# Latent attention: values stationary in the column halves of TensorE, softmax sums by GpSimd

## The chip, the cores and the metric

The kernel runs on one NeuronCore of a Trainium2 chip. Its engines are TensorE (PE in the profile; PEld is its weight load), VectorE (DVE), ScalarE (ACT), GpSimd (POOL) and the sync engine (SP), which here issues the loads of the weights. The metric is the device time of one execution in microseconds.

## The reference, cut to what matters

Two transformer blocks over 512 tokens of width 1024. The change lies in the latent attention of the second block: 16 heads, keys of 64 + 32 features, values of 64, no mask.

```python
def attend(qblk):
    s = jnp.einsum("bqhd,bkhd->bhqk", qblk, kf, preferred_element_type=jnp.float32) * scale
    pr = jax.nn.softmax(s, axis=-1)
    return jnp.einsum("bhqk,bkhd->bqhd", pr.astype(v.dtype), v)
...
o = jnp.moveaxis(o, 0, 1).reshape(bsz, seq, C_HEADS * C_V)
return o @ w_out
```

## The kernel before

Every engine has a program written out by hand in its order, and the engines meet at semaphores. Most matrices are held as a high and a low part (fp32r), and one `product` is three matmuls of 512 columns (L574 to L576). A panel of weights comes in by a DMA, ScalarE writes its high part (`split`, L1343) and VectorE its low part (`low`, L1963).

The latent attention is a loop over 16 heads n; two heads are a pair p. For a head, on TensorE:

- `maxima(n)`: four matmuls q by k (L887), one for each 128 queries. VectorE takes the row maxima (`largest_of`, L2542) and negates them (L2546, semaphore `negm_ready`).
- `turn(n)`: the negated maxima are transposed to a row (L892). VectorE spreads it into four spare rows of q (`shift_of`, L2551, semaphore `shift_ready`), so that the product itself subtracts the maximum.
- `scores(n, kt)`: one product for each of four tiles kt of 128 keys; keys on the partitions, 512 queries in the row. ScalarE takes the exponential into one of four buffers (`weights_of`, L1604).
- `values(n, kt)`: four matmuls (L915). The weights of 128 queries are stationary, the values of the head (64 columns and a column of ones, which gives the softmax sum) move. The result has queries on the partitions.
- VectorE multiplies by the reciprocal of the sum (`result`, L2561 and L2563). For each pair, `turn_pair` transposes four tiles (L925) so that features lie on the partitions; ScalarE and VectorE split that into h_hi and h_lo (`pair_high`, `pair_low`) for the output projection OUT3.

Between these stand the projections of the next heads. In an even head: `project_nope` (three products, then `nope_of` on ScalarE and `nope_lower`, L2942, on VectorE) and `project_k` (two products, then `k_of` and `k_lower`, L2948). In a head with n % 4 == 1: `project_quad` (three products, then `quad_rope`, L2954 to L2957, and in the next head `quad_lower`). GpSimd only copies the rotated parts to their places.

The work of head n + 1 up to its row of maxima is put into head n, so the scores of head n + 1 wait for `shift_ready`, and that waits for the reductions of head n + 1.

## Time and profile before

| | |
|---|---|
| median of 3 runs | 1940.69 us (1940.3 to 1943.07) |
| the profiled execution | 1942.67 us |
| its span, first to last instruction | 1940.8 us |
| mean granted clock of TensorE | 0.987 |
| PE busy | 1887.3 us (97%) |
| DVE busy | 1133.5 us (58%) |
| ACT busy | 737.3 us (38%) |
| POOL busy | 96.6 us (5%) |
| the 16 heads of the latent attention | 1376.5 to 1532.3 us of the span |

The busy time of PE is the union of its instructions; a matmul's record lasts longer than the step to the next one, since matmuls are pipelined. What a matmul costs is read from the starts of two that follow each other. A float32 matmul has two records, an fp32r matmul one. In timelines, "x8" is a run of eight records of one form, and the first two numbers are the start and the length of the run.

### The profile page before, as it was taken

How to read it: one execution, taken by the hardware profiler on the slowest of the kernel's cores; microseconds unless marked ns; L12 is line 12 of the kernel's file. 1: busy time of each engine (PE TensorE's matmuls, PEld its weight loads, DVE VectorE, ACT ScalarE, POOL GpSimd, SP SyncE). 2: the span in 40 equal slices, each digit the busy share in tenths (PEclk: the TensorE clock that was granted, in tenths of full speed). 3: DMA queues.
4: the chain of work that ended last, by engine and by line, in shares of the span. 5: the costliest groups of instructions: out<-in, count | busy, mean ns of one | idle time of the engine just before them, and what ended most of it. 6: DMA issues, size and time to landing. Idle time of an engine off the chain costs nothing.

```text
span 1940.8 us, 25097 instructions
## 1 busy us (share of the span) xinstructions
PE 1887.3 (97%) x9170; PEld 1562.1 (80%) x9170; DVE 1133.5 (58%) x1637; ACT 737.3 (38%) x1074; POOL 96.6 (5%) x123
## 2 busy tenths in 40 slices
PE   8999999999999999999999999999999999999998
PEld 6787778888888887877788888887788878888887
DVE  7767654784764777676543434476767454444344
ACT  5355222542432454554332322343444343323231
POOL 0020000300000020000000000003111000000000
PEclk9998999999999999999999999999999999999999
DMA  5232003233333332311333333332101133232332
GB/s 208 87 128 90 1 20 112 66 96 96 94 95 96 98 109 87 98 55 33 92 92 96 95 97 97 97 97 80 52 22 34 34 97 95 94 96 96 97 98 87
DMA packets 47929, 165.70 MB, mean 85 GB/s; under 512 B 5216, under 2 KB 7264, under 8 KB 47712
## 3 DMA queue, kind: packets, MB, share of 16 engines
q1 hardware_dynamic: 46368, 161.27, 26.3%
q10 hardware_dynamic: 1472, 3.22, 0.5%
q8 instruction: 58, 0.95, 0.2%
q14 instruction: 31, 0.25, 0.0%
HBM read 162.38 MB, written 2.10 MB: 85 GB/s over the span
## 4 chain that ended last, share of the span: by engine, by line
PE 87%; DVE 7%; ACT 2%; POOL 1%; issue 1%; DMA 0%; DVEq 0%; ACTq 0%; POOLq 0%
PE ps L574 26%; PE ps L576 25%; PE ps L575 25%; PE ps L915 3%; PE ps L816 2%; DVE w_lo L1963 1%; POOL x L521 1%; PE ps L1159 1%; PE ps L780 1%; ACT w_hi L1343 1%; PE ps L887 1%; DVE tmp L2000 1%; DVE qk_c L2657 0%; DVE mx L2464 0%; PE ps L1119 0%
## 5 line engine op out<-in xcount | busy, mean ns | idle before, releaser
L1343 ACT ACTIVATE w_hi<-raw 128x1024 fp32r<-128x1024 f32 x281 | 297.7, 1059 | 805.0 <-PE ps L576 804.8
L574 PE MATMUL ps<-h_hi,w_hi 128*128 128x512 f32 (+1 forms) x1288 | 510.5, 396 | 10.7 <-DVE w_lo L1963 9.9
L576 PE MATMUL ps<-h_hi,w_lo 128*128 128x512 f32 (+1 forms) x1288 | 500.1, 388 | 0.0
L575 PE MATMUL ps<-h_lo,w_hi 128*128 128x512 f32 (+1 forms) x1288 | 500.1, 388 | 0.0
L1963 DVE TENSOR_TENSOR w_lo<-raw,w_hi 128x1024 fp32r<-128x1024 f32 x281 | 345.3, 1229 | 126.8 <-ACT w_hi L1343 125.2
L574 PEld LDWEIGHTS ps<-h_hi,w_hi 128*128 128x128 f32 x1288 | 243.5, 189 | 64.5 <-issue 13.9
L575 PEld LDWEIGHTS ps<-h_lo,w_hi 128*128 128x128 f32 x1288 | 243.5, 189 | 50.4 <-issue 2.6
L576 PEld LDWEIGHTS ps<-h_hi,w_lo 128*128 128x128 f32 x1288 | 243.2, 189 | 50.5
L574 PE MATMUL ps<-hid_hi,w_hi 128*128 128x512 f32 (+1 forms) x716 | 273.7, 382 | 1.7 <-DVE w_lo L1963 0.9
L576 PE MATMUL ps<-hid_hi,w_lo 128*128 128x512 f32 (+1 forms) x716 | 272.6, 381 | 0.0
L575 PE MATMUL ps<-hid_lo,w_hi 128*128 128x512 f32 (+1 forms) x716 | 272.6, 381 | 0.0
L2162 DVE TENSOR_TENSOR x<-x,ps 128x512 f32<-128x512 f32 (+2 forms) x82 | 55.3, 674 | 195.6 <-PE ps L576 195.4
L574 PEld LDWEIGHTS ps<-hid_hi,w_hi 128*128 128x128 f32 x716 | 134.6, 188 | 28.8 <-DVE w_lo L1963 2.0
L576 PEld LDWEIGHTS ps<-hid_hi,w_lo 128*128 128x128 f32 x716 | 134.6, 188 | 25.9
L575 PEld LDWEIGHTS ps<-hid_lo,w_hi 128*128 128x128 f32 x716 | 134.6, 188 | 25.8
L2845 DVE SCALAR_TENSOR_TENSOR ev<-ps,tmp 128x512 f32<-128x512 f32 x64 | 44.3, 692 | 161.0 <-PE ps L576 157.1
L915 PEld LDWEIGHTS ps<-mla_v,c_raw 128*128 128x128 f32 x512 | 65.4, 191 | 5.5 <-issue 0.8
L1604 ACT ACTIVATE c_raw<-ps 128x512 f32<-128x512 f32 x64 | 38.2, 597 | 67.9 <-PE ps L576 67.8
L915 PE MATMUL ps<-mla_v,c_raw 128*128 128x65 f32 x512 | 64.0, 268 | 0.0
L1623 ACT ACTIVATE pr<-ps 128x512 f32<-128x512 f32 x48 | 28.1, 597 | 79.8 <-PE ps L806 79.6
L2464 DVE TENSOR_REDUCE mx<-ps 128x1 f32<-128x512 f32 (+4 forms) x52 | 29.8, 587 | 32.9 <-PE ps L784 20.4
L2542 DVE TENSOR_REDUCE mla_mx<-ps 128x1 f32<-128x512 f32 x64 | 41.1, 685 | 13.3 <-PE ps L887 12.8
(381 smaller groups left out, 2379.2 us busy)
## 6 DMA issues: line engine op xcount, KB each, us to landing
raw<-in_panels SPq DMA_DIRECT2D x296, 512.0 KB, 3.5
x_in<-in_x SPq DMA_DIRECT2D x8, 256.0 KB, 5.9
x<-in_x ACTq DMA_DIRECT2D x1, 2048.0 KB, 8.4
out<-y SPq DMA_DIRECT2D x16, 128.0 KB, 1.8
first<-in_first SPq DMA_DIRECT2D x1, 1568.0 KB, 11.8
second<-in_second ACTq DMA_DIRECT2D x1, 512.0 KB, 3.6
small<-in_small ACTq DMA_DIRECT2D x1, 332.0 KB, 4.1
masks<-in_masks SPq DMA_DIRECT2D x1, 256.0 KB, 12.0
```

The costliest lines, as they stand in the source:

```text
L574: nc.tensor.matmul(out, a[0], b[0], start=start, stop=False)
L575: nc.tensor.matmul(out, a[0], b[1], start=False, stop=False)
L576: return nc.tensor.matmul(out, a[1], b[0], start=False, stop=stop)
L816: last = nc.tensor.matmul(ps[:, 6 + n // 6, n % 6 * 65:n % 6 * 65 + 65], pr[:, m % 4, h * P:(h + 1) * P], v, start=w["kt"] == 0 and n in ( ...
L915: last = nc.tensor.matmul(ps[:, mla_bank(n), t * 65:(t + 1) * 65], mla_pr[:, m % 4, t * P:(t + 1) * P], mla_v[:, kt, n, :], start=kt == 0 ...
L1343: nc.scalar.activation(w_high(panel, i), raw[:, panel % 4, :], ACT.Copy).then_inc(w_hi_ready, 1)
L1604: nc.scalar.activation(mla_pr[:, m % 4, :], ps[:, 4 + m % 2, :], ACT.Exp, scale=96 ** -0.5).then_inc(exp_done, 1)
L1963: signal(V.tensor_tensor(w_low(panel, i), raw[:, panel % 4, :], w_high(panel, i).bitcast(F32), ALU.subtract), w_lo_ready, wait=False)
L2162: signal(V.tensor_tensor(x[:, k, at], x[:, k, at], bank, ALU.add), done)
L2464: signal(V.tensor_reduce(mx[:, u["n"] % 2, a:a + r["heads"]], ps[:, 2 + at % 2, 0:r["heads"] * keys].rearrange("p (a b) -> p a b", a=r["he ...
L2542: signal(V.tensor_reduce(mla_mx[:, n % 2, t:t + 1], ps[:, 2 + t % 2, :], AX.X, ALU.max), mx_done, wait=False)
L2845: signal(V.scalar_tensor_tensor(ev[:, k % 4, :], bank, 0.0, inv_b, ALU.max, ALU.mult), tile_out, wait=False)
```

## The change

For a pair and a key tile, four matmuls now hold the values (128 keys by 64 features) stationary and let the weights of 256 queries move. The first head of the pair writes partitions 0 to 63 of the result (column half 0 of the array), the second partitions 64 to 127. The result has features on the partitions at once, so `turn_pair` and the column of ones go. The softmax sums come another way: GpSimd adds the four weight tiles of each head (three additions of 128x512), `totals(p)` multiplies the sum by a stationary block of ones (four matmuls, which spread it over 64 partitions), and VectorE turns that by blocks, takes 16 reciprocals for each partition and turns them back (`shares`), then multiplies (`pair_result`). Weights have eight buffers. `values` of a pair runs in its odd head and, for the last key tile, in the next even head. In even heads `turn` stands before the last scores.

```diff
-        def values(n, kt):
-            m = 4 * n + kt
-            pe.wait_ge(exp_done, m + 1)
-            if kt == 0 and n >= 2:
-                pe.wait_ge(o_used, n - 1)
-            for t in range(NT):
-                last = nc.tensor.matmul(ps[:, mla_bank(n), t * 65:(t + 1) * 65], mla_pr[:, m % 4, t * P:(t + 1) * P],
-                                        mla_v[:, kt, n, :], start=kt == 0 and t == 0, stop=kt == NT - 1, skip_group_check=True)
+        def values(p, kt):
+            pe.wait_ge(exp_done, 4 * (2 * p + 1) + kt + 1)
+            if kt == 0 and p >= 2:
+                pe.wait_ge(pair_out, p - 1)
+            for half in range(2):
+                for a in range(2):
+                    n = 2 * p + a
+                    last = nc.tensor.matmul(ps[64 * a:64 * a + 64, pair_bank(p), cols_of(half)], mla_v[:, kt, n, :],
+                                            weights_tile(n, kt)[:, cols_of(half)], start=kt == 0 and half == 0, stop=kt == NT - 1,
+                                            skip_group_check=True)
             last.then_inc(pv_done, 1)
-        def turn_pair(p):
-            pe.wait_ge(o_used, 2 * p + 2)
+        def totals(p):
+            pe.wait_ge(weights_added, 6 * p + 6)
             pe.wait_ge(k_low, min(2 * p + 6, HEADS))
             if p:
-                pe.wait_ge(mix_ready, 8 + p)
-            for t in range(NT):
-                last = nc.tensor.transpose(ps[:, 1, t * P:(t + 1) * P], mla_out[:, p % 2, t, :], ident)
-            last.then_inc(turned, 1)
+                pe.wait_ge(totals_taken, p)
+            for half in range(2):
+                for a in range(2):
+                    last = nc.tensor.matmul(ps[64 * a:64 * a + 64, 1, cols_of(half)], ones[:, 0:64],
+                                            weights_sum(2 * p + a)[:, cols_of(half)], start=half == 0, stop=True, skip_group_check=True)
+            last.then_inc(totals_out, 1)
...
+        def add_weights(n):
+            if n >= 4:
+                pool.wait_ge(totals_out, n // 2 - 1)
+            for kt in range(1, NT):
+                pool.wait_ge(exp_done, 4 * n + kt + 1)
+                nc.gpsimd.tensor_tensor(weights_sum(n), weights_tile(n, 0) if kt == 1 else weights_sum(n), weights_tile(n, kt),
+                                        ALU.add).then_inc(weights_added, 1)
+                pool.wait_ge(weights_added, 3 * n + kt)
...
+            if even and p:
+                values(p - 1, 3)
             scores(n, 1)
             if even and p + 1 < PAIRS:
                 project_nope(p + 1)
-            values(n, 0)
+            if not even:
+                values(p, 0)
             if more:
                 maxima(n + 1, range(2, 4))
             scores(n, 2)
-            if even and p + 1 < PAIRS:
-                project_k(p + 1)
-            if not even and p:
-                turn_pair(p - 1)
-            values(n, 1)
-            scores(n, 3)
-            if more:
-                turn(n + 1)
-            if n % 4 == 1 and p + 2 < PAIRS:
-                project_quad(p // 2 + 1)
-            values(n, 2)
+            if even:
+                if p + 1 < PAIRS:
+                    project_k(p + 1)
+                turn(n + 1)
+                scores(n, 3)
+            else:
+                if p:
+                    totals(p - 1)
+                values(p, 1)
+                scores(n, 3)
+                if more:
+                    turn(n + 1)
+                if n % 4 == 1 and p + 2 < PAIRS:
+                    project_quad(p // 2 + 1)
+                values(p, 2)
...
+            if n >= 2:
+                act.wait_ge(pv_done, 4 * (n // 2 - 1) + kt + 1)
+                act.wait_ge(weights_added, 3 * (n - 2) + max(1, kt))
...
+        def shares(p):
+            dve.wait_ge(totals_out, p + 1)
+            signal(V.transpose(mla_total, ps[:, 1, :]), totals_taken)
+            link(V.reciprocal(mla_w[:], mla_total[:, 0:S:32]))
+            signal(V.transpose(mla_share, mla_w[:].unsqueeze(2).to_broadcast([P, 16, 32])), dve_step)
+
+        def pair_result(p):
+            dve.wait_ge(pv_done, 4 * p + 4)
+            if p >= 2:
+                dve.wait_ge(mix_ready, 8 + p - 1)
+            signal(V.tensor_tensor(mla_out[:, p % 2, :], ps[:, pair_bank(p), :], mla_share, ALU.mult), pair_out, wait=False)
...
-            if n:
-                result(n - 1)
+            if even and p >= 2:
+                pair_low(p - 2)
...
             if not even and p:
-                pair_low(p - 1)
+                shares(p - 1)
+                pair_result(p - 1)
```

On ScalarE, `pair_high(p - 1)` moves behind the last exponential of an odd head, ahead of the `split` of the next panel. At the end of the loop, `totals` of the last pair stands inside the first tile of OUT3, and the second tile is begun before the first one's last product.

In TensorE's program, the end of head 6 and the first instruction of head 7 stood so before; the first two rows are the values of key tile 1, L892 is `turn(7)`, and the last row is the first product of head 7:

```order
L915 MATMUL ps<-mla_v,c_raw 128x65 [waits exp_done]
L915 MATMUL ps<-mla_v,c_raw 128x65 x3
L574 MATMUL ps<-q_hi,k_hi 128x512 [waits exp_done]
L575 MATMUL ps<-q_lo,k_hi 128x512
L576 MATMUL ps<-q_hi,k_lo 128x512
L892 MATMUL ps<-small,mla_negm 4x128 [waits negm_ready]
L915 MATMUL ps<-mla_v,c_raw 128x65 [waits exp_done]
L915 MATMUL ps<-mla_v,c_raw 128x65 x3
L574 MATMUL ps<-q_hi,k_hi 128x512 [waits shift_ready,rope_placed,exp_done,k_low,nope_low]
```

After the change (L598 to L600 is the product, L916 is `turn`), the first two rows are the end of `project_k(4)`:

```order
L599 MATMUL ps<-cq_lo,w_hi 128x512
L600 MATMUL ps<-cq_hi,w_lo 128x512
L916 MATMUL ps<-small,mla_negm 4x128 [waits negm_ready]
L598 MATMUL ps<-q_hi,k_hi 128x512 [waits exp_done]
L599 MATMUL ps<-q_lo,k_hi 128x512
L600 MATMUL ps<-q_hi,k_lo 128x512
L598 MATMUL ps<-q_hi,k_hi 128x512 [waits shift_ready,rope_placed,exp_done,k_low,nope_low]
L599 MATMUL ps<-q_lo,k_hi 128x512
```

Both visits of the values have left the end of the even head, and one product stands between `turn` and the scores that wait for its result.

In VectorE's program, this stood from head 5 (n % 4 == 1) to the second half of head 6 before; L2567 is `pair_low(1)`, L2954 to L2957 `quad_rope`, L1963 the low part of a panel:

```order
L2567 TENSOR_TENSOR h_lo<-ps,h_hi 128x512 [waits turned_high]
L2954 STREAM_SHUFFLE c_t<-ps 128x512 [waits quad_low,quad_proj]
L2955 TENSOR_TENSOR c_t<-ps,trig 128x512 [waits dve_step]
L2956 TENSOR_TENSOR c_t<-c_t,trig 128x512 [waits quad_taken]
L2957 TENSOR_TENSOR c_t<-c_t 128x512 [waits dve_step]
L1963 TENSOR_TENSOR w_lo<-raw,w_hi 128x1024 [waits w_hi_ready,quad_done]
L2542 TENSOR_REDUCE mla_mx<-ps 128x1 [waits mx_ready] x2
L2963 TENSOR_TENSOR quad_lo<-c_t,quad_hi 128x512 [waits rope_placed,quad_high]
L2561 RECIPROCAL mla_w<-ps 128x4 [waits pv_done]
L2563 TENSOR_TENSOR ang<-ps,mla_w 128x4x64 [waits dve_step]
L2942 TENSOR_TENSOR q_lo<-ps,q_hi 64x512 [waits nope_high,o_used]
L2942 TENSOR_TENSOR q_lo<-ps,q_hi 64x512 [waits nope_high]
```

After the change, the same place (L2605 to L2607 are `shares(1)`, L2614 is `pair_result(1)`, L2618 `pair_low`):

```order
L2605 STREAM_TRANSPOSE sq<-ps 128x512 [waits totals_out]
L2606 RECIPROCAL mla_w<-sq 128x16 [waits totals_taken]
L2607 STREAM_TRANSPOSE sq<-mla_w 128x512 [waits dve_step]
L2614 TENSOR_TENSOR ang<-ps,sq 128x512 [waits pv_done,dve_step]
L3005 STREAM_SHUFFLE c_t<-ps 128x512 [waits quad_low,quad_proj]
L3006 TENSOR_TENSOR c_t<-ps,trig 128x512 [waits dve_step]
L3007 TENSOR_TENSOR c_t<-c_t,trig 128x512 [waits quad_taken]
L3008 TENSOR_TENSOR c_t<-c_t 128x512 [waits dve_step]
L2010 TENSOR_TENSOR w_lo<-raw,w_hi 128x1024 [waits w_hi_ready,quad_done]
L2589 TENSOR_REDUCE mla_mx<-ps 128x1 [waits mx_ready] x2
L3014 TENSOR_TENSOR quad_lo<-c_t,quad_hi 128x512 [waits rope_placed,quad_high]
L2618 TENSOR_TENSOR h_lo<-ang,h_hi 128x512 [waits pair_high_ready]
```

Four instructions of 512 columns or fewer now stand ahead of `quad_rope` in the place of `pair_low`, and `pair_low` has taken the place of the two of `result`.

## Rows read from the trace of the kernel before

**Rows 1.** busy times of the stage (engine busy us, instructions; PEclk: granted clock).
```profile
1376.50:1532.30 155.80, 153.32 (x942) 133.51 (x943) 105.55 (x184) 67.25 (x110) 18.22 (x25) 1.00 0.10 31
```

**Rows 2.** waits in the stage: us in total, times, longest.
```profile
PEld ps L574 <- issue: 3.0, 12, 0.3
```

**Rows 3.** timeline of PE, one `values` visit and the product behind it.
```profile
1435.72 1.00 PE L915 MATMUL ps<-mla_v,c_raw 128*128 128x65 f32 x8
1436.53 0.48 PE L574 MATMUL ps<-q_hi,k_hi 128*128 128x512 f32 x1
1436.85 0.39 PE L575 MATMUL ps<-q_lo,k_hi 128*128 128x512 f32 x1
1437.08 0.40 PE L576 MATMUL ps<-q_hi,k_lo 128*128 128x512 f32 x1
```

**Rows 4.** groups by form, whole span: float32 matmuls with 512 and 256 columns.
```profile
L749 PE MATMUL ps<-ret_pr,rv 128*128 128x512 f32 x8 | 4.1, 591 | 0.0
...
L749 PE MATMUL ps<-ret_pr,rv 128*128 128x256 f32 x8 | 2.4, 378 | 0.0
```

**Rows 5.** timeline of PE where 64-row matmuls stand between 128-row ones.
```profile
817.72 0.39 PE L576 MATMUL ps<-w_hi,h_lo 128*128 128x512 f32 x1
818.04 0.46 PE L1107 MATMUL ps<-small,la 64*128 64x64 f32 x4
...
818.59 1.07 PE L1119 MATMUL ps<-neg_m,small 64*128 64x512 f32 x2
819.60 0.50 PE L574 MATMUL ps<-h_hi,w_hi 128*128 128x512 f32 x1
```

**Rows 6.** timeline of PE, the four transposes of `turn_pair`.
```profile
1452.60 0.60 PE L925 MATMUL ps<-small,ang 128*128 128x128 f32 x4
1453.03 1.00 PE L915 MATMUL ps<-mla_v,c_raw 128*128 128x65 f32 x8
```

**Rows 7.** timeline, all engines: head 0 behind its `project_nope`.
```profile
1380.48 1.00 PE L915 MATMUL ps<-mla_v,c_raw 128*128 128x65 f32 x8
...
1382.74 1.29 DVE L2542 TENSOR_REDUCE mla_mx<-ps 128x1 f32<-128x512 f32 x2
...
1384.07 0.17 DVE L2546 TENSOR_SCALAR mla_negm<-mla_mx 128x4 f32<-128x4 f32 x1
```

**Rows 8.** timeline, all engines: from `turn` to the next head's scores.
```profile
1446.45 0.27 PE L892 MATMUL ps<-small,mla_negm 128*4 128x128 f32 x1
...
1446.76 0.68 DVE L2551 TENSOR_TENSOR q_hi<-ps,small 4x512 fp32r<-4x512 f32 x1 [0.39 <-PE ps L892]
...
1447.73 0.47 PE L574 MATMUL ps<-q_hi,k_hi 128*128 128x512 f32 x1 [0.17 <-issue]
```

**Rows 9.** timeline of DVE, from `quad_rope` to the second pair of maxima.
```profile
1395.64 0.73 DVE L2954 STREAM_SHUFFLE c_t<-ps 128x512 f32<-128x512 f32 x1
...
1398.58 1.23 DVE L1963 TENSOR_TENSOR w_lo<-raw,w_hi 128x1024 fp32r<-128x1024 f32 x1
1399.72 1.28 DVE L2542 TENSOR_REDUCE mla_mx<-ps 128x1 f32<-128x512 f32 x2
1400.92 0.68 DVE L2963 TENSOR_TENSOR quad_lo<-c_t,quad_hi 128x512 fp32r<-128x512 f32 x1
...
1402.19 1.41 DVE L2942 TENSOR_TENSOR q_lo<-ps,q_hi 64x512 fp32r<-64x512 f32 x2
1403.63 1.29 DVE L2542 TENSOR_REDUCE mla_mx<-ps 128x1 f32<-128x512 f32 x2
```

**Rows 10.** one line's instructions on GpSimd: duration ns min/median/max.
```profile
L521 POOL TENSOR_TENSOR x<-x,tmp x32: 723/916/929, 339.1 to 728.3; 128x256 f32<-128x256 f32 x32
```

**Rows 11.** one line's instructions on VectorE: duration ns min/median/max.
```profile
L1963 DVE TENSOR_TENSOR w_lo<-raw,w_hi x281: 1209/1225/1572, 7.7 to 1918.0; 128x1024 fp32r<-128x1024 f32 x141
```

**Rows 12.** busy times of two stretches around a fall of the clock.
```profile
170.00:175.00 5.00, 3.25 (x27) 2.79 (x25) 3.01 (x4) 3.01 (x6) 0.00 (x0) 1.00 0.58 204
175.00:180.00 5.00, 4.91 (x14) 2.55 (x12) 4.02 (x7) 2.90 (x6) 0.00 (x0) 0.51 0.33 105
```

More of the change, by code:

```diff
@@ L532, in _ @@
         pool.wait_ge(inv_copied, COPIED_BEFORE["c"] + 1)
-        alone(nc.gpsimd.memset(mla_v[:, :, :, 64:65], 1.0))
         alone(nc.gpsimd.memset(k_hi[:].bitcast(F32), 0.0))
@@ L554, in _, with place_two @@
             alone(nc.gpsimd.tensor_copy(k_lo[rope_rows(n), n, :], k_lo[rope_rows(n), n - 2, :]))
-        for i in range(HEADS // 4):
-            for first in (0, 2):
-                pool.wait_ge(quad_high, i + 1)
-                if i and first:
-                    pool.wait_ge(s_ready, 16 * i)
-                for n in (first, first + 1):
-                    place(q_hi[rope_rows(n), n, :], quad_hi[32 * n:32 * n + 32, :])
-                pool.wait_ge(quad_low, i + 1)
-                for n in (first, first + 1):
-                    place(q_lo[rope_rows(n), n, :], quad_lo[32 * n:32 * n + 32, :])
+        def place_two(i, first):
+            pool.wait_ge(quad_high, i + 1)
+            if i and first:
+                pool.wait_ge(s_ready, 16 * i)
+            for n in (first, first + 1):
+                place(q_hi[rope_rows(n), n, :], quad_hi[32 * n:32 * n + 32, :])
+            pool.wait_ge(quad_low, i + 1)
+            for n in (first, first + 1):
+                place(q_lo[rope_rows(n), n, :], quad_lo[32 * n:32 * n + 32, :])
+        def add_weights(n):
[6 more added lines that the diff above has]
+                pool.wait_ge(weights_added, 3 * n + kt)
+        place_two(0, 0)
+        place_two(0, 2)
+        for n in range(HEADS):
+            if n % 4 == 2 and n + 2 < HEADS:
+                place_two(n // 4 + 1, 0)
+            add_weights(n)
+            if n % 4 == 3 and n + 1 < HEADS:
+                place_two(n // 4 + 1, 2)
         inverse_root("ffn2")
@@ L862, in project_k @@
             if p >= 3:
-                pe.wait_ge(mix_ready, 8 + p - 2)
+                pe.wait_ge(totals_taken, p - 2)
             for k in range(2):
@@ L891, in turn @@
             pe.wait_ge(negm_ready, n + 1)
-            nc.tensor.transpose(ps[0:4, mla_bank(n), 384:512], mla_negm[:, n % 2, :], ident).then_inc(negm_turned, 1)
+            nc.tensor.transpose(ps[0:4, 2, 0:P], mla_negm[:, n % 2, :], ident).then_inc(negm_turned, 1)
         def scores(n, kt):
@@ L1243, in _ @@
             dense(panel, moving=(aq_hi, aq_lo))
-        def out_run(panel, base, most):
-            for k in range(KD):
-                dense(panel + k, freed=k == KD - 1, **(dict(ready=mix_ready, base=base, most=most) if k == 0 else {}))
         def feed_forward(panel, base, hidden, name, halved=None):
@@ L1305, in _ @@
                 maxima(n + 1, range(0, 2))
-            if n:
-                values(n - 1, 3)
+            if even and p:
+                values(p - 1, 3)
             scores(n, 1)
@@ L1314, in _, with out_part @@
             scores(n, 2)
-            if even and p + 1 < PAIRS:
-                project_k(p + 1)
-            if not even and p:
-                turn_pair(p - 1)
-            values(n, 1)
-            scores(n, 3)
-            if more:
-                turn(n + 1)
-            if n % 4 == 1 and p + 2 < PAIRS:
-                project_quad(p // 2 + 1)
-            values(n, 2)
-        values(HEADS - 1, 3)
-        turn_pair(PAIRS - 1)
-        out_run(OUT3, 8, 16)
+            if even:
+                if p + 1 < PAIRS:
+                    project_k(p + 1)
+                turn(n + 1)
+                scores(n, 3)
[9 more added lines that the diff above has]
+                values(p, 2)
+        values(PAIRS - 1, 3)
+        def out_part(panel, ks):
+            pe.wait_ge(w_lo_ready, panel + 1)
+            pe.wait_ge(tile_out, output_of(panel) - 3)
+            for k in ks:
+                pe.wait_ge(mix_ready, 8 + k + 1)
+                last = product(ps[:, bank_at(panel), :], w(panel, k * P, (k + 1) * P), (h_hi[:, k, :], h_lo[:, k, :]), k == 0, k == KD - 1)
+                if k == KD - 1:
+                    last.then_inc(panel_read, 1)
+        out_part(OUT3, range(0, 2))
+        totals(PAIRS - 1)
+        out_part(OUT3, range(2, KD - 1))
+        out_part(OUT3 + 1, range(0, KD // 2))
+        out_part(OUT3, range(KD - 1, KD))
+        out_part(OUT3 + 1, range(KD // 2, KD))
+        for panel in range(OUT3 + 2, OUT3 + KD):
+            dense(panel, freed=panel == OUT3 + KD - 1)
         feed_forward(FF2, 0, sum(FF0_CHUNKS) + 8 * FF_CHUNKS, "ffn2", halved="final")
@@ L2998, in _ @@
                 low(pair_panel(p + 3))
-        result(HEADS - 1)
+        pair_low(PAIRS - 2)
+        shares(PAIRS - 1)
+        pair_result(PAIRS - 1)
         pair_low(PAIRS - 1)
```

58 lines of the change are left out of this document (25 added, 33 removed).

## The prediction

> **What bounds the kernel now.** I read first the busy times of the stage: from the first scores of head 0 to OUT3, PE is busy 153.3 of 155.8 us at a granted clock of 1.00, VectorE 105.6, ScalarE 67.3, GpSimd 18.2 [rows 1]. So PE sets the end, and any PE work that goes is gained, as long as the chains on the other engines still fit under it. The waits show where they nearly don't: twelve times PE's weight load for L574 is held up [rows 2]. One such place: after `turn` the matrix result reaches VectorE 0.31 us later, `shift_of` takes 0.68, and the next head's first product starts 0.29 us after that, 1.28 us after `turn` in all [rows 8]. The values visit in between fills only 0.11 + 0.81 us [rows 3], so each of the twelve costs about 0.36 us, 4.3 in all. The stage is PE bound with a latency chain just under its surface.
>
> **PE work removed.** A values visit takes 0.81 us to the next start, and the product behind it takes one step of 0.32 where 0.23 is usual [rows 3]: 0.90 us, times 64 is 57.6. `turn_pair` takes 0.43 [rows 6] and the same 0.09, times 8 is 4.2. Together 61.8 us.
>
> **PE work added.** There are 32 new visits and 8 `totals`, each four float32 matmuls of 256 columns, eight records. A record of such a matmul lasts 378 ns at 256 columns and 591 at 512 [rows 4]; the difference says that 256 columns stream for 0.213 us. Neighbouring matmuls write different column halves, and nothing before runs two halves of the array at once, so this cost is bounded: all eight in a row are 1.71 us, two halves fully side by side 0.85. In between, if records start in program order, the second record of one matmul runs beside the first of the next: five slots, 1.07. I take 1.07, since the two records of one matmul share a half and PE's records start in order in every timeline that I read. Then the change of tile shape: the one place with another shape is 64 rows, where the first L1107 starts 0.32 after L576 instead of 0.23; the last L1119 streams until about 819.50 (818.59 + 1.07 - 0.59 + 0.43) and L574 starts at 819.60 [rows 5]. That is 0.09 in and 0.09 out, and 0.09 on the product behind as today: 0.28. The other end is 0.09, since the 4-column L892 shows no step [rows 8]. I take 1.35 us a visit: 40 x 1.35 = 54.0. **PE work: 54.0 - 61.8 = -7.8 us** (side by side -16.6, in a row +17.8).
>
> The Trainium skill (TensorEngine Tiling (Array Packing), Tiling Modes, Key Properties) says that different tiles can execute LdWeights and Matmul in parallel, but that changing the mode drains the engine. By its first half alone the saving would be nearer 16.6, by its second each visit pays both ways. The 64-row rows agree with a price of the mode change, 0.09 each way; no row shows two tiles in parallel.
>
> **Waits added in even heads.** This is what speaks against the change. The visits of key tiles 0, 1 and 2 have left the even heads, where the longest chain is. In head 0 the last `project_nope` matmul gives way at 1380.48; then ScalarE, `nope_lower`, two reductions and the negation follow, until 1384.07 + 0.17 [rows 7], 3.76 us, and 0.29 to PE [rows 8]: 4.05. Ahead of `turn` PE had 0.46 + 0.69 + 1.38 us and two visits and a product, 5.0 in all. Now it has 2.53. PE stands 1.5 us at `turn` in heads 0 and 2.
> From head 4 on VectorE is the longer one. From its `shift_of` in an odd head to the next negation it does (steps between starts): `shift_of` 0.71 [rows 8], `shares`, `pair_result` 0.72, `quad_rope` 2.94, low part 1.14, reductions 1.20, `quad_lower` 0.68, `pair_low` 0.72, `nope_lower` 1.44 [rows 9], reductions and negation 1.50 [rows 7]. A block transpose is in no row: I take the shuffle's 0.76 [rows 9], between 0.5 and 1.5, twice, and 0.2 for the reciprocal, 1.72. Sum 12.8, with 0.31 and 0.29 at the ends 13.4. PE in the same stretch: `turn` 0.11, `project_quad` 2.07, two visits 2.70, three products 2.07, `project_nope` 2.07, four maxima 0.92, `project_k` 1.38, 11.3. Wait 2.05, in heads 6 and 10.
> In heads 4, 8 and 12 there is no `quad_rope` and `quad_lower`; but there the low part waits about 1.7, since ScalarE's `split` now stands behind `pair_high`, which waits for `pair_result`: VectorE 11.4, PE 9.25, wait 2.2. Head 14 has no projections: 10.0 against 5.8, wait 4.2. Sum: 3.0 + 4.1 + 6.6 + 4.2 = 17.9.
> Behind `turn` the even head has one product, 0.69. Reckoned from the negation, `k_lower` 0.71, `shift_of` 0.71 and 0.29 stand against 0.29 + 0.11 + 0.69: 0.6 in 8 heads, 4.8. Odd heads have the visit of 1.35 there, which covers 1.28. From 22.7 the 4.3 of before go, and 0.7 at the end of the loop, where `turn_pair` stood alone behind `result` and OUT3 now fills in. **Waits: +17.7 us.**
>
> **GpSimd.** Its addition of 256 columns takes 0.92 us [rows 10]; 512 columns are at most 1.83, at least 1.3. Three for a head and 1.2 us of placements are 6.7 of the 10 us that a head takes, so `totals`, a head and a half later, doesn't wait; behind it on PE stand a visit and the last scores. ScalarE's new waits for GpSimd lie two heads back. But the low part took up to 1.57 us instead of 1.23 [rows 11], the longest ones beside GpSimd's copies. VectorE has 5.9 us of operations with two SBUF inputs in four heads (two low parts, two of `quad_rope`, `quad_lower`, two of `pair_low`); 28% of it, for the 60% of the time that GpSimd works, is 4 us in the stage, of which I put 2.5 on the path (0 to 4.7).
>
> **Sum:** -7.8 + 17.7 + 2.5 = +12.4 us. The profiled execution took 1942.67, 1.9 more than its span and 2.0 more than the median of the runs, so it gives 1955.1, and on the median **1953 us**. A difference of 0.2% (3.9 us) is what can be told from none.
>
> **Rivals.**
> - Halves in a row (0.25): the eight records don't overlap. Visits of 1.99, PE +17.8; VectorE has more time, and every even head's wait falls to the 1.5 of heads 0 and 2 (12, and about 1 in head 14) beside the 4.8: 18, net +13. 1940.7 + 30.8 + 1.5 is 1973. For it: no row shows an overlap. Against: the halves share neither weights nor results.
> - Fully side by side (0.18): PE -16.6, but VectorE bounds six of the even heads, and each waits 0.44 more (two visits): 25.3, net +20.3. With 2.5 for GpSimd, 1947.
> - The clock falls (0.13): the granted clock went to about 0.5 in a stretch behind 5 us in which PE was busy 3.25 [rows 12], and around `turn` in an even head PE will be busy 0.8 of about 3.2 us (1.8 and 0.6 waited). 3.3 us at half speed lose 1.65; eight times is 13: 1966. Against: it is one place, and the odd heads between stay dense.
> - GpSimd becomes the bound (0.05): from additions of about 2.5 us; at 3.0 `totals` waits 5 us more in all: 1958.
> - Not slower (0.12): side by side and no price for the mode change. A visit costs 0.85 + 0.09 = 0.94, PE saves 24, and the waits of net 22 eat it: 1939 to 1943. Faster by over 0.2% it gets below 0.80 us a visit, or where the transposes take 0.5 (2.7 us less) and GpSimd disturbs nothing: 1936.
>
> **How the numbers follow.** The forecast has 0.27, with its own range 1949 to 1961 (transposes, disturbance, mode change). Slower is it and the first four rivals with nearly all of their chance, 0.87; the last splits into 0.06 same and 0.06 faster, and 0.01 of the side-by-side case is same. The range runs from the side-by-side case less 3 us to the serial one plus 3: 1944 to 1976; outside are the last rival and the tails.
>
> **What would show it.** The start of a visit to the next instruction: 1.26 (1.07 and the way in and out), or 1.9 or 0.95, for the halves. Waits of PE's `turn` (L916) for VectorE's negation of 11 us or more and of the maxima (L911) for VectorE's reductions of some 5 us; L598 held for `shift_of` in every even head, never in an odd one. VectorE's busy share in the stage above 70%; additions on GpSimd of 1.5 to 1.8 us; no wait of PE for GpSimd. The stage, 155.8 us before, should last about 168. The forecast is wrong if the visits are not bound by streaming 256 columns, if the clock falls, or if VectorE's stretch between `shift_of` and the negation is not 13 us.

## The result: 0.5% slower, and the profile after

| | before | after |
|---|---|---|
| median | 1940.69 us (5 runs, 1939.11 to 1944.22) | 1950.70 us (5 runs, 1949.65 to 1952.65) |
| ratio | 1 | 1.005, 95% interval 1.0036 to 1.0065 |
| span of the profiled execution | 1940.8 us | 1950.7 us |
| first scores of head 0 to OUT3 | 155.8 us | 164.3 us |

The forecast was 1953 (1944 to 1976), slower with a chance of 0.87. The attention stage grew by 8.5 us, which is nearly the whole difference. The stretch of [rows 1] is now this one (busy us and instructions for PE, PEld, DVE, ACT and POOL, PEclk, DMA share, GB/s):

```profile
1376.40:1540.70 164.30, 145.01 (x711) 90.83 (x711) 113.61 (x180) 66.92 (x110) 77.34 (x73) 0.97 0.10 29
```

PE is busy for 145.0 us of the stage, 8.3 less than before, and it stands idle for 19.3 us where it was 2.5. VectorE has 8.1 us more to do (it is busy for 69% of the stage, where the forecast had said above 70%), GpSimd 59. The granted clock is 0.97 where it was 1.00. PE's work did shrink; what it gave back, and more, went into waits.

**A visit.** Timeline of PE in the kernel after, one visit of `values` with the products around it (start, length, line):

```profile
1533.82 0.39 PE L600 MATMUL ps<-q_hi,k_lo 128*128 128x512 f32 x1
1534.14 0.43 PE L941 MATMUL ps<-c_raw,mla_v 128*64 128x256 f32 x1
1534.14 0.43 PE L941 MATMUL ps<-ev,mla_v 128*64 128x256 f32 x1
1534.40 0.38 PE L941 MATMUL ps<-c_raw,mla_v 128*64 128x256 f32 x1
1534.41 0.38 PE L941 MATMUL ps<-ev,mla_v 128*64 128x256 f32 x1
...
1534.84 0.38 PE L941 MATMUL ps<-c_raw,mla_v 128*64 128x256 f32 x1
1534.84 0.38 PE L941 MATMUL ps<-ev,mla_v 128*64 128x256 f32 x1
1535.15 0.50 PE L598 MATMUL ps<-q_hi,k_hi 128*128 128x512 f32 x1
1535.49 0.40 PE L599 MATMUL ps<-q_lo,k_hi 128*128 128x512 f32 x1
```

The records of the two heads (c_raw and ev) start at the same moment. The next pair starts 0.26 us later, the two behind it (one is left out above) at steps of 0.22, where [rows 4] gave 0.213 for the stream of 256 columns. Eight records take four slots, not the five that I took and not eight. From the first record to the next product are 1.01 us. Around it L941 starts 0.32 behind L600 instead of 0.23, and L599 0.34 behind L598 instead of 0.23: a visit costs 1.01 + 0.09 + 0.11 = 1.21 us.

**The waits.** PE and its weight load in the stage (us in total, times, the longest):

```profile
PE ps L916 <- DVE mla_negm L2593: 11.0, 8, 2.5
...
PE ps L598 <- DVE q_hi L2598: 4.7, 8, 1.0
PE ps L911 <- DVE mla_mx L2589: 4.0, 5, 2.5
...
PEld ps L954 <- POOL tmp L577: 1.8, 5, 0.4
```

Forecast were 17.9 us at `turn` and the maxima together, and 4.8 for `shift_of` (L598). The rows say 11.0 + 4.0 and 4.7. One of the eight waits of L598, the longest with 0.98 us, ends where the stage begins (1376.42) and stood there before the change too; in the stage are seven, 3.7 us.

These rows count idle time, from the end of one record to the start of the next. What a wait costs is more, since the last record lasts longer than its step. One of the waits of `turn`:

```profile
1403.41 0.39 PE L600 MATMUL ps<-cq_hi,w_lo 128*128 128x512 f32 x1
1405.24 0.27 PE L916 MATMUL ps<-small,mla_negm 128*4 128x128 f32 x1 [1.44 <-DVE mla_negm L2593]
```

L916 starts 1.83 us behind L600, where 0.23 is usual: the wait costs 1.60, not 1.44. Counted so over the timeline of the stage, from start to start as the forecast had them, `turn` waits 12.3 us, the maxima 6.6 (the second matmul of a pair is late too) and `shift_of` 4.9, 23.8 in all.

**What was not in the sum: a held negation.** The instructions of one line of the kernel after, the negation of 128x4 maxima (ns: shortest, median, longest):

```profile
L2593 DVE TENSOR_SCALAR mla_negm<-mla_mx x16: 169/170/1178, 1374.6 to 1530.2; 128x4 f32<-128x4 f32 x16
```

Three of the fifteen in the stage are long, 0.45, 1.18 and 1.18 us. A timeline of one of the two longest, cut to GpSimd's addition (L577), the negation and `turn` (L916):

```profile
1447.56 1.26 POOL L577 TENSOR_TENSOR tmp<-tmp,c_raw 128x512 f32<-128x512 f32 x1
1447.67 1.18 DVE L2593 TENSOR_SCALAR mla_negm<-mla_mx 128x4 f32<-128x4 f32 x1
...
1448.90 0.27 PE L916 MATMUL ps<-small,mla_negm 128*4 128x128 f32 x1 [2.49 <-DVE mla_negm L2593]
```

And the chain through it, in order of time:

```profile
1443.79 0.60 DVE quad_lo L3014
1444.39 0.60 DVE h_lo L2618
1444.99 0.59 DVE q_lo L2993
...
1445.62 0.69 DVE q_lo L2993
...
1446.34 1.30 DVE mla_mx L2589 x2
...
1447.67 1.18 DVE mla_negm L2593
```

GpSimd's addition starts at 1447.56 and lasts 1.26 us, to 1448.82. The negation starts 0.11 us later and ends at 1448.85. `turn` (L916), which had been held for 2.49 us, starts at 1448.90. In the kernel with shorter additions (below) no negation of the stage takes more than 172 ns. The chain shows what else stands ahead of it, all VectorE: the low parts of the rotated q, the pair and the next q (L3014, L2618, L2993), two reductions, the negation.

The Trainium skill (SBUF — State Buffer, Who interferes with whom) says that a `tensor_scalar` of VectorE in a mode that uses two ports excludes GpSimd and is excluded by it for a whole instruction, whichever starts first. The row agrees: the negation ends 0.03 us after the addition. No row shows which mode it ran in.

**And the clock.** Three stretches of the stage, the same columns as above:

```profile
1403.00:1407.20 4.20, 2.22 (x10) 1.27 (x9) 4.07 (x7) 1.96 (x4) 2.30 (x3) 1.00 0.00 0
1407.20:1410.70 3.50, 3.50 (x12) 2.21 (x12) 1.30 (x3) 1.20 (x2) 1.06 (x1) 0.51 0.02 5
1445.00:1450.00 5.00, 2.38 (x11) 1.31 (x9) 4.87 (x7) 1.87 (x4) 3.60 (x4) 1.00 0.10 39
```

In 1403.0 to 1407.2 PE was busy for 2.22 of 4.2 us; then the granted clock was 0.51, the lower of its two levels (1.2 of 2.4 GHz), for 3.5 us, which costs 1.7. In 1445 to 1450 PE was busy for 2.38 of 5 us and the clock stayed. Four heads later the same wait of 2.49 us came again, behind the same work (2.39 of 5 us in 1487.1 to 1492.1), and there the clock fell, at 1492.6. So a long wait can bring a fall, but whether one comes can't be told from these rows. In all it fell three times in the stage, 5.1 us; before, never.

### The profile page after: what moved, and what is told of

It reads as the page before. It is cut to its first block, busy times and chain, and to the rows that moved or that the text cites. A ratio compares the mean times of both kernels' runs of the same rounds, so it can differ in the third digit from the quotient of the medians.

```text
span 1950.7 us, 24721 instructions
## 1 busy us (share of the span) xinstructions
PE 1880.6 (96%) x8946; PEld 1519.6 (78%) x8946; DVE 1144.8 (59%) x1637; ACT 737.2 (38%) x1074; POOL 155.8 (8%) x170
## 4 chain that ended last, share of the span: by engine, by line
PE 84%; DVE 11%; ACT 2%; issue 2%; POOL 1%; DMA 0%; DVEq 0%; ACTq 0%; POOLq 0%
PE ps L598 25%; PE ps L600 24%; PE ps L599 24%; PE ps L840 2%; DVE w_lo L2010 1%; PE ps L941 1%; ACT w_hi L1389 1%; DVE mla_mx L2589 1%; POOL x L527 1%; PE ps L1189 1%; PE ps L804 1%; PE ps L911 1%; DVE tmp L2047 1%; DVE q_lo L2993 0%; DVE qk_c L2708 0%
## 5 line engine op out<-in xcount | busy, mean ns | idle before, releaser
L598 PE MATMUL ps<-h_hi,w_hi 128*128 128x512 f32 (+1 forms) x1288 | 510.8, 397 | 10.5 <-DVE w_lo L2010 9.7
L599 PE MATMUL ps<-h_lo,w_hi 128*128 128x512 f32 (+1 forms) x1288 | 500.3, 388 | 0.0
L600 PE MATMUL ps<-h_hi,w_lo 128*128 128x512 f32 (+1 forms) x1288 | 500.2, 388 | 0.0
L598 PEld LDWEIGHTS ps<-h_hi,w_hi 128*128 128x128 f32 x1288 | 243.4, 189 | 65.8 <-issue 14.5
L600 PEld LDWEIGHTS ps<-h_hi,w_lo 128*128 128x128 f32 x1288 | 243.2, 189 | 50.5
L599 PEld LDWEIGHTS ps<-h_lo,w_hi 128*128 128x128 f32 x1288 | 243.5, 189 | 50.0 <-issue 2.6
L598 PE MATMUL ps<-hid_hi,w_hi 128*128 128x512 f32 (+1 forms) x716 | 273.6, 382 | 1.7 <-DVE w_lo L2010 0.9
L599 PE MATMUL ps<-hid_lo,w_hi 128*128 128x512 f32 (+1 forms) x716 | 272.6, 381 | 0.0
L600 PE MATMUL ps<-hid_hi,w_lo 128*128 128x512 f32 (+1 forms) x716 | 272.6, 381 | 0.0
L598 PEld LDWEIGHTS ps<-hid_hi,w_hi 128*128 128x128 f32 x716 | 134.6, 188 | 29.0 <-DVE w_lo L2010 2.0
L600 PEld LDWEIGHTS ps<-hid_hi,w_lo 128*128 128x128 f32 x716 | 134.6, 188 | 25.8
L599 PEld LDWEIGHTS ps<-hid_lo,w_hi 128*128 128x128 f32 x716 | 134.6, 188 | 25.6
L2896 DVE SCALAR_TENSOR_TENSOR ev<-ps,tmp 128x512 f32<-128x512 f32 x64 | 44.3, 692 | 161.1 <-PE ps L600 157.2
L500 POOL TENSOR_TENSOR r<-r,small 128x2 f32<-128x2 f32 x6 | 4.2, 701 | 893.4 <-DVE r L2100 893.4
L495 POOL TENSOR_TENSOR r<-r,small 128x4 f32<-128x4 f32 x8 | 8.1, 1015 | 517.7 <-DVE r L2053 517.7
L598 PE MATMUL ps<-w_hi,h_hi 128*128 128x512 f32 (+1 forms) x128 | 47.1, 368 | 1.5 <-DVE w_lo L2010 1.5
```

The lines of the kernel that those rows point to most:

```text
L598: nc.tensor.matmul(out, a[0], b[0], start=start, stop=False)
L599: nc.tensor.matmul(out, a[0], b[1], start=False, stop=False)
L600: return nc.tensor.matmul(out, a[1], b[0], start=False, stop=stop)
L2896: signal(V.scalar_tensor_tensor(ev[:, k % 4, :], bank, 0.0, inv_b, ALU.max, ALU.mult), tile_out, wait=False)
```

## The experiments

All times are medians; the kernel before ran beside each group of four, at 1940.8 to 1941.1. The stage is read from each profiled execution, as above, and varies less than the whole (no edit touches what is ahead of it, and yet it starts anywhere from 1371.9 to 1377.0). It is one execution for each kernel, and so is the number of falls.

| kernel | median us | ratio to before, 95% | stage us | clock falls in the stage |
|---|---|---|---|---|
| before | 1940.69 | 1 | 155.8 | 0 |
| after | 1950.70 | 1.0050 (1.0036 to 1.0065) | 164.3 | 3 |
| shares first | 1943.76 | 1.0015 (1.0006 to 1.0024) | 157.2 | 1 |
| visit ahead of `turn` | 1950.09 | 1.0050 (1.0038 to 1.0062) | 163.4 | 3 |
| split first | 1951.80 | 1.0056 (1.0044 to 1.0068) | 167.5 | 7 |
| all reordered | 1932.84 | 0.9959 (0.9947 to 0.9971) | 147.6 | 0 |
| few additions | 1945.31 | 1.0021 (1.0012 to 1.0031) | 157.7 | 1 |
| half twice | 1950.60 | 1.0047 (1.0030 to 1.0064) | 166.0 | 4 |
| before, small maxima | 1939.30 | 0.9996 (0.9986 to 1.0006) | 155.8 | 0 |
| after, small maxima | 1939.57 | 0.9987 (0.9977 to 0.9996) | 152.0 | 1 |
| one half | 1975.36 | 1.0181 (1.0164 to 1.0198) | 189.2 | 2 |
| shares and split first | 1942.42 | 1.0013 (1.0002 to 1.0024) | 157.2 | 1 |
| reordered, few additions | 1931.95 | 0.9953 (0.9937 to 0.9970) | 144.9 | 0 |
| before, spare additions | 1940.49 | 1.0000 (0.9990 to 1.0010) | 155.8 | 0 |

A fall lasts 3.4 us and costs 1.7; one of twice that length counts as two. The theory: PE saves some 15 us, and in the even heads the chain of VectorE's operations up to the negation eats it. The rivals: GpSimd's additions, the clock, or a saving on PE that isn't there.

### Does PE save what the timeline says?

**Half twice.** In a visit both matmuls of one head stand ahead of both of the other:

```diff
-            for half in range(2):
-                for a in range(2):
+            for a in range(2):
+                for half in range(2):
```

> In a values visit the loops are exchanged: both 256-column matmuls of one head, then both of the other, so that neighbouring matmuls use the same column half of the array except in the middle. Theory (two halves stream together only where neighbouring matmuls alternate between them): a visit costs some 0.4 to 0.8 us more, 32 visits 13 to 25 us of PE work, partly in stretches that wait anyway, time 1958 to 1970. Rival (PE looks further ahead, or the side by side doesn't matter): 1951.

Measured 1950.60, the rival; the stage is longer by the 1.7 us of one more fall. The timeline of PE shows why:

```profile
1410.41 0.38 PE L941 MATMUL ps<-c_raw,mla_v 128*64 128x256 f32 x1
1410.42 0.43 PE L941 MATMUL ps<-ev,mla_v 128*64 128x256 f32 x1
1410.63 0.38 PE L941 MATMUL ps<-c_raw,mla_v 128*64 128x256 f32 x1
1410.69 0.38 PE L941 MATMUL ps<-ev,mla_v 128*64 128x256 f32 x1
...
1411.43 0.50 PE L598 MATMUL ps<-q_hi,k_hi 128*128 128x512 f32 x1
```

In the code, both matmuls of `c_raw` (four records) stand ahead of the first of `ev`. Yet the first record of `ev` starts 0.01 us behind the first of `c_raw`, and the visit still takes 1.02 us. The two halves stream side by side in either order, so PE's records don't start in the order of the program across the halves. That was the reason for my five slots, and it is wrong. The Trainium skill (TensorEngine Tiling (Array Packing), Tiling Modes, Key Properties) says that different tiles can execute in parallel; both orders agree, with starts 0.00 to 0.06 us apart.

**One half.** Both heads are written to the same 64 rows of the bank (so the output mixes the two heads):

```diff
-                    last = nc.tensor.matmul(ps[64 * a:64 * a + 64, pair_bank(p), cols_of(half)], mla_v[:, kt, n, :],
+                    last = nc.tensor.matmul(ps[0:64, pair_bank(p), cols_of(half)], mla_v[:, kt, n, :],
...
-                    last = nc.tensor.matmul(ps[64 * a:64 * a + 64, 1, cols_of(half)], ones[:, 0:64],
+                    last = nc.tensor.matmul(ps[0:64, 1, cols_of(half)], ones[:, 0:64],
```

> Both heads of a pair are written to the same 64 rows of the bank, so that all matmuls of values and totals use one column half of the array; their number and shapes are those of the change. The output isn't the reference's: two heads are added up in one half, and the other is stale. Theory (the change's PE work is short because the two halves stream at the same time): the eight records of a visit start 0.215 us apart, the visit takes 2.0 us instead of 1.2, 40 visits are 32 us more PE work, of which some 8 to 14 fill stretches in which PE waits for VectorE now; time 1968 to 1975. Rival (the overlap doesn't come from the two halves): 1950 to 1952.

Measured 1975.36, 24.7 above the change and just above the expected range. A visit of it:

```profile
1409.30 0.65 PE L941 MATMUL ps<-c_raw,mla_v 128*64 128x256 f32 x2
1409.78 0.59 PE L941 MATMUL ps<-ev,mla_v 128*64 128x256 f32 x2
1410.21 0.59 PE L941 MATMUL ps<-c_raw,mla_v 128*64 128x256 f32 x2
1410.64 0.59 PE L941 MATMUL ps<-ev,mla_v 128*64 128x256 f32 x2
1411.17 0.73 PE L911 MATMUL ps<-k_hi,q_hi 128*128 128x512 f32 x2
```

Now the eight records follow each other and the visit takes 1.87 us, 0.86 more than 1.01. The stage holds 39 of the 40 (the last `totals` stands in OUT3), so 33.5 us. Shorter waits take 6.1 back (17.7 us from start to start instead of 23.8) and one fall of the clock fewer 1.7, which leaves 25.7; the stage grew by 24.9. So the overlap is worth 0.86 us a visit, and it comes from the two halves.

**Small maxima, before and after.** The row maxima are taken over 32 of the 512 columns, and the exponent's scale is 0.001 instead of 0.102 so that nothing overflows (the output isn't the reference's). That shortens VectorE's chain by some 2 us a head and leaves PE's work alone:

```diff
-                signal(V.tensor_reduce(mla_mx[:, n % 2, t:t + 1], ps[:, 2 + t % 2, :], AX.X, ALU.max), mx_done, wait=False)
+                signal(V.tensor_reduce(mla_mx[:, n % 2, t:t + 1], ps[:, 2 + t % 2, 0:32], AX.X, ALU.max), mx_done, wait=False)
```

> The kernel before with the row maxima taken over 32 of the 512 columns and the exponent's scale made 0.001 instead of 0.102, so that no exponential overflows; the output isn't the reference's. VectorE's chain is shorter by about 2 us a head, PE's work is the same. Theory: before, the chain was already hidden, so 1938 to 1941.

> The change with the same two cuts (row maxima over 32 of 512 columns, exponent's scale 0.001; the output isn't the reference's). Theory (VectorE's chain eats the change's saving of about 15 us on PE): the wait of L916 falls from 11.0 to some 5 us and this runs at or below the kernel before with the same cut: from 4 below it to 1 above, 1936 to 1941. Rival (PE saves little or nothing, as my sum's 7.8, or GpSimd costs it): it stays 5 us or more above the kernel before with the same cut.

The kernel before hardly moves (its stage is 155.8 us with and without), the change gains 11.1 us and is level with it: 1939.57 and 1939.30. In the stage it is 3.7 us ahead. The wait of `turn` fell from 11.0 to 6.3. Of the 12.3 us that the stage gained, 3.4 are two falls of the clock fewer, the rest waits. So there is a saving on PE, and VectorE's chain stood on it; before, that chain was covered.

### Which order loses it?

**Shares first.** In odd heads VectorE does the sums of the last pair and its result ahead of `shift_of`:

```diff
+            if not even and p:
+                shares(p - 1)
+                pair_result(p - 1)
...
-            if not even and p:
-                shares(p - 1)
-                pair_result(p - 1)
```

> Only VectorE's order changes: in odd heads the sums' transposes and the product with the values (shares, pair_result) stand ahead of shift_of for the next head, not behind it. Theory (VectorE's chain in the even heads eats PE's saving): shift_of is the first thing that VectorE does after the odd head's maxima and the rest of the chain to the next negation is VectorE's, so the 2.3 us of shares and pair_result come off it wherever VectorE had been idle ahead of shift_of; the wait of L916 falls from 11.0 to 3 to 6 us, a new wait of L598 for shift_of in odd heads takes up to 1 us back, and the time is about 1944 to 1946, 5 to 6 us below the change. Rival (GpSimd's additions slow VectorE, or the clock falls set the loss): the order doesn't matter and the time stays at 1950 to 1951.

Measured 1943.76, 6.9 less. The total is about right, what makes it up is not what I had expected (PE's waits, in the stage):

```profile
PE ps L916 <- DVE mla_negm L2593: 10.6, 8, 1.8
...
PE ps L598 <- DVE q_hi L2598: 6.4, 12, 0.6
...
PE ps L911 <- DVE mla_mx L2589: 0.3, 1, 0.3
```

`turn` still waits 10.6 us; it is the wait for the maxima that fell from 4.0 to 0.3, and two of the three falls of the clock went, which is 3.4 of the 7.1 us that the stage gained; the waits, from start to start, gave 2.8. The reason is in VectorE's row of `nope_lower` (L2993; the last numbers are its idle time ahead of it and what ended it), first of the change with two rows that are used below, then of this kernel:

```profile
L2010 DVE TENSOR_TENSOR w_lo<-raw,w_hi 128x1024 fp32r<-128x1024 f32 x9 | 12.0, 1335 | 6.7 <-ACT w_hi L1389 6.6
...
L2993 DVE TENSOR_TENSOR q_lo<-ps,q_hi 64x512 fp32r<-64x512 f32 x14 | 9.6, 686 | 3.4 <-ACT q_hi L1928 3.2
...
L2593 DVE TENSOR_SCALAR mla_negm<-mla_mx 128x4 f32<-128x4 f32 x15 | 4.8, 323 | 0.5
```

```profile
L2993 DVE TENSOR_TENSOR q_lo<-ps,q_hi 64x512 fp32r<-64x512 f32 x14 | 9.6, 689 | 10.6 <-ACT q_hi L1928 10.4
```

VectorE now waits 10.4 us there for ScalarE's high part, which waits for PE's own `project_nope`. With VectorE early, the second chain shows: PE, ScalarE, VectorE and back to `turn`, the 1.5 us a head that I had reckoned for heads 0 and 2. Two chains of nearly one length end at `turn`. PE's timeline agrees: `turn` waits 1.15 or 1.16 us in heads 0, 4, 8 and 12 of this kernel, and as long in each of heads 0 to 12 of one half, where PE's own work is longer so what is left there hangs on PE's own work, as the chain through ScalarE does, and not on VectorE alone.

**Visit ahead of `turn`.** In even heads `values(p - 1, 3)` moves from behind the first scores to behind `project_k`:

```diff
-            if even and p:
-                values(p - 1, 3)
...
+                if p:
+                    values(p - 1, 3)
```

> Only PE's order changes: in even heads the visit of key tile 3 goes from behind the first scores to behind project_k, right ahead of the turn. Theory: six of the eight waits are VectorE's length, not PE's, so a visit of 1.2 us put ahead of the turn fills the wait but what stood behind it is missed there, and PE is left to wait for shift_of behind the turn: L916 falls by 7 to 9 us, the wait of L598 grows by about as much, time 1949 to 1951. Rival (the wait at the turn is lost for want of work on PE there): 8 x 1.2 = up to 9 us gained, 1941 to 1943.

Measured 1950.09, no gain. PE's waits in the stage:

```profile
PE ps L911 <- DVE mla_mx L2589: 10.5, 7, 3.7
...
PE ps L916 <- DVE mla_negm L2593: 4.1, 3, 1.5
```

`turn` waits 6.9 us less, and the maxima for VectorE's reductions 6.5 us more. The maxima's second pair stands ahead of `turn`, and the visit had stood ahead of that pair. Without it PE comes to the pair 1.2 us earlier, while VectorE is as late as before: PE meets it there (L911), a step earlier in the head, where I had expected it behind `turn` (L598).

**Split first.** ScalarE splits the next panel ahead of `pair_high`, which waits for VectorE:

```diff
-            if not even and p:
-                pair_high(p - 1)
             if not even and p + 3 <= PAIRS + 1:
                 split(pair_panel(p + 3))
+            if not even and p:
+                pair_high(p - 1)
```

> Only ScalarE's order changes: the split of the next weight panel stands ahead of pair_high (which waits for VectorE's pair_result) in odd heads, not behind it. Theory (chain of VectorE, with its low part late in heads 4, 8, 12 and tight elsewhere): the low part on VectorE no longer waits for the split, L916 falls by 3 to 5 us, time 1946 to 1948. Rival (the split isn't what VectorE waits for): within 1 us of 1950.7.

> Two of the reorderings together: shares and pair_result ahead of shift_of (VectorE), and the split of the next panel ahead of pair_high (ScalarE). Alone the first gave -7 us, with one fall of the clock in its profiled execution, and the second +1 us, with seven falls. Theory (the second shortens the chain too, but alone it left a pattern of waits behind which the clock fell seven times): together 1936 to 1941, with two falls or fewer. Rival (the split wasn't what VectorE waits for): within 1.5 us of the first alone, 1942 to 1945.

Alone 1951.80, 1.1 more than the change; with the shares first 1942.42, against 1943.76 for these alone, intervals that overlap. Both theories fail: no 3 to 5 us came, nor 1936 to 1941. Alone, PE's waits of the three kinds fell a little, from 19.7 to 17.8 us, but `turn` waits more, not less:

```profile
PE ps L916 <- DVE mla_negm L2593: 13.1, 8, 2.5
```

In heads 4, 8 and 12 the wait for the maxima went, so the split was what VectorE had waited for there, and that of `turn` rose from 0.88 to the 1.16 us of the other chain: nearly nothing was left to gain. And the clock fell seven times instead of three in the profiled execution (the longest of its six), 6.8 us more. Here is one of them, in a place where it had held in the change:

```profile
1445.00:1450.00 5.00, 1.99 (x9) 1.06 (x8) 4.87 (x7) 1.78 (x3) 3.01 (x4) 1.00 0.01 3
1450.00:1453.80 3.80, 3.80 (x14) 2.39 (x14) 1.37 (x3) 1.19 (x2) 1.13 (x1) 0.55 0.00 0
```

PE was busy for 1.99 of 5 us ahead of this fall, 2.38 in the change, where it held. That is no rule: with few additions (below) the one fall came behind 5 us with 2.42. With the shares first there was one fall, and the stage is 157.2 us with or without the split.

**All reordered.** These three, and both `k_lower` behind `shift_of`, and `pair_low` at the end of VectorE's work in an even head:

```diff
-            if even and p >= 2:
-                pair_low(p - 2)
...
-            if even and p + 1 < PAIRS:
-                k_lower(2 * p + 2)
...
+                k_lower(2 * p + 2)
...
+            if even and p >= 2:
+                pair_low(p - 2)
```

> All the reorderings together: the visit ahead of the turn, shares and pair_result ahead of shift_of in odd heads, split ahead of pair_high, both k_lower behind shift_of, pair_low at the end of VectorE's work in even heads. No work is added or taken away. Theory (the change saves PE some 15 us by its halves running side by side, and the order of VectorE and PE around the turns loses them again): the waits of L916 and L911 together fall from 15 to under 5 us and the time is 1932 to 1937, below the kernel before (1940.7). Rival (GpSimd's additions and the clock take it): the sum of the waits hardly changes or comes up elsewhere, 1945 or more.

Measured 1932.84, 17.9 below the change and 8 below the kernel before (ratio 0.9959). Its stage in busy times, and PE's waits in it:

```profile
1374.00:1521.60 147.60, 139.66 (x712) 88.59 (x712) 115.93 (x180) 67.26 (x110) 79.41 (x72) 1.00 0.11 33
```

```profile
PE ps L598 <- DVE q_hi L2598: 4.7, 12, 0.6
...
PE ps L916 <- DVE mla_negm L2593: 1.2, 1, 1.2
...
PE ps L911 <- DVE mla_mx L2589: 0.6, 1, 0.6
```

The same work in another order takes 147.6 us: the waits at `turn` and the maxima are 1.8 us instead of 15.0, all of PE's idle time is 7.9 instead of 19.3, and the clock never fell, which is 5.1 of the 16.7 us that the stage gained. The gains don't add up one by one: -6.9, -0.6 and +1.1 alone, -17.9 together. Shares first uncovers the chain through ScalarE, and the visit alone meets VectorE's. But moving `k_lower` and `pair_low` was not tried by itself, so how much is theirs, and how much comes of moving both chains at once, stays open.

### What do GpSimd's additions cost?

**Few additions.** GpSimd adds 32 of the 512 columns (the sums, and so the output, are incomplete), once in the change and once in the reordered kernel:

```diff
+                few = slice(0, 32)
-                nc.gpsimd.tensor_tensor(weights_sum(n), weights_tile(n, 0) if kt == 1 else weights_sum(n), weights_tile(n, kt),
+                nc.gpsimd.tensor_tensor(weights_sum(n)[:, few], (weights_tile(n, 0) if kt == 1 else weights_sum(n))[:, few],
...
```

> GpSimd adds only 32 of the 512 columns of every weights tile, so the sums, and with them the output, are incomplete; every other instruction is as in the change. Theory (the order of VectorE's and PE's work sets the loss): GpSimd doesn't bound and hardly disturbs, the time stays within 1.5 us of 1950.7 and VectorE's operations with two SBUF inputs keep their means. Rival (my 2.5 us for GpSimd's disturbance of VectorE, up to 4.7): 1946 to 1948.5, and the low parts on VectorE get shorter by up to 0.3 us each.

> All reorderings, with GpSimd adding only 32 of the 512 columns (the sums and the output are incomplete). With the change's own order this cut gave -5.4 us. Theory (GpSimd's additions hold up VectorE, which costs time only where PE waits for VectorE): with the waits mostly gone the cut gives 0 to 2 us, 1931 to 1933. Rival (GpSimd costs time in another way, on PE or by its own lateness): 3 us or more, below 1930.

In the change's order 1945.31, 5.4 less: the rival, and more than its upper end. VectorE's rows (lines are one further down here):

```profile
L2011 DVE TENSOR_TENSOR w_lo<-raw,w_hi 128x1024 fp32r<-128x1024 f32 x9 | 11.0, 1225 | 7.3 <-ACT w_hi L1390 7.1
...
L2594 DVE TENSOR_SCALAR mla_negm<-mla_mx 128x4 f32<-128x4 f32 x15 | 2.6, 170 | 0.5
```

The negation falls from 323 ns in the mean to 170, the low part from 1335 to 1225, 3.3 us in all, and `turn` waits 8.3 us instead of 11.0; in each of heads 6 and 10 it waits 1.46 instead of 2.49. The stage is 6.5 us shorter: about 3.3 are PE's waits (20.5 us from start to start instead of 23.8), 3.4 are two falls of the clock fewer. In the reordered kernel the cut gives 0.9 us in the median, with intervals that overlap, and 2.7 in the stage: less, as the theory has it.

**Before, with spare additions.** The kernel before, with GpSimd adding spare tiles in place, three in each of heads 0 to 11, between its copies of the rotated parts as in the change:

```diff
+            for kt in range(1, NT):
+                pool.wait_ge(exp_done, 4 * n + kt + 1)
+                alone(nc.gpsimd.tensor_tensor(tmp[:, n % 4, :], tmp[:, n % 4, :], tmp[:, (n + 1) % 4, :], ALU.add))
```

> The kernel before, with GpSimd doing 36 additions of 128x512 float32 (three in each of heads 0 to 11, as the change has them, when the exponentials are done) of spare tiles in place; nothing reads the results. Theory (they lengthen VectorE's operations, but before VectorE is hidden behind PE): VectorE's low parts and negations get longer, the time rises by 0 to 1.5 us, 1940.5 to 1942.5. Rival (the disturbance reaches PE in any order): 3 us or more, 1944 and above.

Measured 1940.49, no change. VectorE's rows show the same disturbance, without a price:

```profile
L1977 DVE TENSOR_TENSOR w_lo<-raw,w_hi 128x1024 fp32r<-128x1024 f32 x9 | 12.4, 1375 | 0.4
...
L2560 DVE TENSOR_SCALAR mla_negm<-mla_mx 128x4 f32<-128x4 f32 x15 | 5.9, 393 | 0.5
```

The negation takes 393 ns in the mean where it took 170, the low part 1375 where it took 1351. PE doesn't wait for either, and the stage is 155.8 us as before: nothing is lost.

## Why the prediction was right, and what in it was wrong

The sign, the place and the mechanism held: PE's work shrinks, the visits leave the even heads, and PE stands at `turn` behind VectorE. That the total came out only 2.3 us below the forecast is luck: PE saved 7.7 us more than forecast, and the clock, which was not in the sum, took 5.1. The prediction itself had named a fall of the clock as a sign that it is wrong.

- **PE work.** Forecast -7.8 from 1.35 us a visit. Measured: 40 visits of 1.21, less 2.8 where two stand side by side (seven times `totals` and a visit, once the last two visits) and share the change of shape, are 45.6. Of the 61.8 removed, 0.7 was counted twice: behind `turn_pair` stands a visit [rows 6], whose product behind was reckoned already. 61.1 - 45.6 is 15.5. (The steps of the two timelines, waits and slow stretches left out, add up to 15.8 less in the stage.) The step that failed is "I take 1.07, since the two records of one matmul share a half and PE's records start in order": it is four slots, in either order of the code. The way in and out was right: 0.09 and 0.10, and 0.11 behind, for 0.09 each.
- **Waits at `turn` and the maxima.** Forecast 17.9, measured 18.9 from start to start. The stretch of VectorE was the right one: from `turn(6)` to `turn(7)` it never rests for more than 35 ns, and it takes 13.9 us where 13.4 was forecast, 1.0 of it the held negation. The block transposes took 0.72 and 0.71 us for the assumed 0.76. Heads 0 and 2 waited 1.3 and 1.6 for the forecast 1.5. But in the other heads the chain through ScalarE is nearly as long, which the sum didn't show and only the shares first did.
- **`shift_of` in even heads.** Forecast 4.8 in eight heads, measured 4.9 from start to start in seven, none in an odd head. In head 14 it didn't wait.
- **GpSimd.** Forecast +2.5 from low parts that get 28% longer. They didn't: 1335 ns in the mean, 1351 before. The negation did, by 2.3 us in 15, in the chain; the cut of the additions puts the price in PE's waits at 3.3. A price of about the right size in another operation. Additions take 1.27 us, just below my lower bound of 1.3:

```profile
L577 POOL TENSOR_TENSOR tmp<-tmp,c_raw x16: 1262/1272/1299, 1382.6 to 1532.8; 128x512 f32<-128x512 f32 x16
```

- **The clock.** A rival with 0.13 and a price of 13 us for eight falls. Three came, 5.1 us. It belonged in the sum as a part of the likeliest case, since it hangs on the very waits that I forecast.
- **Rivals.** Halves in a row would have been 1973 by my sum; made so, the kernel takes 1975.36. "Fully side by side" was the true case for PE, with 1947 against 1950.70: short by the clock. GpSimd never became the bound: the weight load of `totals` waited 1.8 us for it, but the steps of PE there are the usual 0.32 us.

With the measured sizes the sum is -15.5 - 4.3 - 0.7 + 18.9 + 4.9 + 5.1 = 8.4 us, and the stage grew by 8.5; the single terms are good to half a microsecond or so. GpSimd's price is inside the waits.

## What to carry to other kernels

A saving on the busiest engine moves work away from where it covered a chain: before counting it, go through the loop with the new order and see what stands ahead of each short wait. Where two chains of nearly equal length end at one instruction, undoing one shows less than it is worth; move both before judging. And count a wait from start to start: the idle time in a row leaves out what the last record hides. A small operation in a chain (here 128x4) can be held for as long as a large one of GpSimd lasts, so GpSimd's work is better put where that chain isn't running (not tried here).

## What was not expected of the hardware

Matmuls into the two column halves start in pairs, 0 to 0.06 us apart, even where the code has two of one half in a row (four records), and a pair takes the 0.21 to 0.22 us of one. The negation of 128x4 values lasted 1.18 us beside an addition of GpSimd and ended 0.03 us after it. The granted clock fell to half behind waits of PE, three times in the stage, but not behind each: after the wait of 2.49 us in head 6 it held, after the same one in head 10 it fell. The reordered kernel, with the same work, had no fall there.
